# One PSUM bank for the modulation fold, others for gathers and a norm sum, and a reordered router stage, in a two-block transformer kernel on one core

## The chip, the core and the metric

The kernel runs as one program on one core of a Trainium2 chip. The metric is the device time of one execution in microseconds (us); lower is better. TensorE multiplies into eight PSUM banks of 128 partitions by 512 float32 values, VectorE, ScalarE and GpSimd work beside it, and weights are brought from HBM by DMA transfers, nearly all of them issued in order from one queue (SyncE's, "SPq" in the profile). In the profile PE is TensorE's matmul, PEld its weight load, DVE is VectorE, ACT is ScalarE, POOL is GpSimd.

## The reference

Two transformer blocks on 256 tokens of width 1024, then a norm. The change lies wholly in the first block, in two places of it: the attention and the router.

```python
mod = jax.nn.silu(c) @ w_ada[l] + b_ada[l]
shift1, scale1, gate1, shift2, scale2, gate2 = jnp.split(mod[:, None, :], 6, axis=-1)
...
y_na = neighbourhood_attention(qa, ka, va, na_rpb[l])
...
y_mla = blocked_full_attention(qm, km, vm)
...
x = x + gate1 * (merged @ w_out[l])
h2 = rms_norm(x, g_norm2[l]) * (1.0 + scale2) + shift2
# moe_ffn: 64 experts, 8 chosen for each token
scores = jax.nn.sigmoid((t @ w_router).astype(jnp.float32))
...
routed = lax.map(expert_chunk, (tc, gc)).reshape(T, D)
shared = (jax.nn.silu(t @ w_sg) * (t @ w_su)) @ w_sd
```

The modulation `mod` is a product of one vector with a 1024 x 6144 matrix; the experts' weights are 64 times three 1 MB matrices.

## The kernel before

Each engine's program is written out by hand, one function for each engine, and each engine runs its own program strictly in order. Nothing is scheduled by a planner: the order in the code is the order on the engine. What ties the engines together are semaphores.

**Banks.** `open_group(name, b)` on TensorE waits until the bank `b` has been emptied by whoever reads its last group, and takes it. `close_group` marks the group full, `full(engine, name)` makes an engine wait for that, and `emptied(instruction, name)` gives the bank back. So a bank number is a wait: a group opened in a bank whose last reader is late stops TensorE, and all that is queued behind it. `done(engine, name)` waits for the same release.

**Weights.** A ring of 11 slots of 1 MB holds weight slabs. `take_slab` waits for the next one; `ends(n, group)` says with which group's end a slot is free, and SyncE's queue then issues the next load into it. The loads are in one fixed order. The slabs of the experts that are sorted by load come after a wait for `ordered`, which VectorE sets once it has copied out the sorted list of experts (L2331). The first two expert units and the slabs before them don't need it.

**Attention** (`early_attention`, L637 to L671). `scores(0)`, `ada_fold(1)`, `scores(1)`, four slabs of modulation product (L493, 16 instructions each), and then eight times: scores two pairs ahead (L610), two transposes `turn` of the probabilities (L626), two more slabs of modulation product, and the values product of the pair before (L640). Each pair is two heads. `ada_fold` (L520 to L526) turns a quarter-summed row of the modulation into columns with four short matmuls. The scores of pair 0 go to banks 0 and 1, those of pair 1 to banks 5 and 7, those of pair 2 to 0 and 1 again. VectorE takes for every head the row maximum of the scores (`na_scores`, L2167 and L2172), and later scales the exponentials by their sum (L2097, L2100). Its own order is: maxima of pair 0, `ada(1)` (L1983, which reads the fold and frees its bank), maxima of pair 1, scaling of pair 0, maxima of pair 2, scaling of pair 1, and so on. GpSimd makes the bias of each head ahead of its maximum (L1545): that of head h starts when the scores of head h - 2 have been read.

**Router** (L926 to L1034 on TensorE, L2237 to L2375 on VectorE). The router's logits are summed in `rtT`, copied out transposed (`rtS`, L2240) and turned back (`rt`, bank 7, L949 and L951). `row_sums` gives each token's norm, `two_sums` (L543, L545) gives the same sums broadcast over partitions (`sum2`). `turn_rows` (`tk`, four groups in banks 1 to 4) turns the activations for the gathers; VectorE empties them in `rest_of` (L2252, 0.7 us each). From the sigmoid scores VectorE works out the mask of the chosen experts (L2256 to L2285), the counts, the sorting matrix `perm`, the list of experts, and each token's place. `shared("shg", ...)` is the gate product of the shared expert, 16 steps in two groups: banks 0 and 7. It depends on none of the sorting and stands between the sorting's short matmuls. `gather(0, 0)` to `gather(0, 3)` (L1021) fetch the tokens of the first two expert units, and ScalarE evicts them (L1792). `unit(0)` starts the experts; its first group `gu` opens bank 5 (L1189).

## Time and profile before

| | us |
|---|---|
| three timed runs | 1097.80, 1099.66, 1099.83 |
| their median | 1099.66 |
| the profiled execution's own time | 1099.61 |
| its span in the profile | 1097.8 |
| mean granted TensorE clock | 0.991 of full |

The span is 1.8 us shorter than the time of the same execution; that rest lies around the span and is taken as fixed. The page of the profile shows PE busy for 1055.3 us of the span, DVE 394.4, ACT 286.6, POOL 54.0, and DMA at 421 GB/s in most slices between 329 and 823 us. In a timeline row the columns are start, length, engine, line, operation, output and inputs, shape, count, and in brackets the idle time before it and what released it. Float32 matmuls show twice in such a row: a product of two float32 tiles counts two.

### The profile page before, as it was taken

The page shows a single profiled execution, that of the slowest core. Times are in us where ns is not written, and L with a number is a line of the kernel's source. Part 1 is how long each engine was busy: PE and PEld are TensorE (multiplying, and loading weights), DVE is VectorE, ACT ScalarE, POOL GpSimd, SP SyncE. Part 2 cuts the span into 40 slices and gives each one's busy share as a digit, 9 for nine tenths or more (in the row PEclk, how much of TensorE's full clock was granted, in tenths as well). Part 3 has the DMA queues.
Part 4 walks back from the last instruction along what each step waited for, and adds up shares of the span by engine and source line. Part 5 has one row for each costly group of instructions (what it writes and reads, how often), then busy time and mean ns, then how long its engine had stood idle before and what let it go on. Part 6 is the DMA issues. An engine that isn't in the chain of part 4 may idle for free.

```text
span 1097.8 us, 15950 instructions
## 1 busy us (share of the span) xinstructions
PE 1055.3 (96%) x6296; PEld 726.0 (66%) x6296; DVE 394.4 (36%) x1034; ACT 286.6 (26%) x658; POOL 54.0 (5%) x87
## 2 busy tenths in 40 slices
PE   6999999999999998999899999999889999999998
PEld 4786775688755654665356655655458888887567
DVE  1298976523532232112112122122333021523841
ACT  3124145511431121122111121113222111213951
POOL 0000202013100000000000000001000001100001
PEclk9999999999999999999989999999999999999999
DMA  9999387965599999999999999999997334310000
GB/s 384 338 420 421 148 349 283 421 261 194 213 350 423 421 420 420 420 421 420 421 420 421 407 421 421 420 421 421 418 417 282 125 116 154 115 39 1 1 2 38
DMA packets 49611, 335.12 MB, mean 305 GB/s; under 512 B 5472, under 2 KB 7872, under 8 KB 9984
## 3 DMA queue, kind: packets, MB, share of 16 engines
q1 hardware_dynamic: 46976, 329.01, 73.7%
q10 hardware_dynamic: 2176, 3.37, 1.0%
q0 software_dynamic: 384, 1.70, 0.4%
q8 instruction: 51, 0.84, 0.3%
q14 instruction: 24, 0.20, 0.0%
HBM read 333.02 MB, written 1.05 MB: 304 GB/s over the span
## 4 chain that ended last, share of the span: by engine, by line
PE 90%; DMA 4%; DVE 4%; ACT 1%; issue 1%; SPq 0%; DVEq 0%; ACTq 0%
PE bank L1189 14%; PE bank L574 10%; PE bank L1232 7%; PE bank L1144 5%; PE bank L1331 5%; PE bank L1021 4%; DMA ring<-experts 4%; PE bank L1043 3%; PE bank L493 3%; PE bank L1081 3%; PE bank L1419 3%; PE bank L901 3%; PE bank L1374 3%; PE bank L917 3%; PE bank L704 2%; PE bank L640 2%
## 5 line engine op out<-in xcount | busy, mean ns | idle before, releaser
L1189 PE MATMUL bank<-ring,arena 128*32 128x512 f32 (+1 forms) x1112 | 176.9, 605 | 11.3 <-DMA ring<-experts 10.7
L1189 PEld LDWEIGHTS bank<-ring,arena 128*32 128x32 f32 (+1 forms) x1112 | 52.3, 121 | 115.4 <-issue 115.3
L574 PE MATMUL bank<-hT,ring 128*128 128x256 f32 x512 | 113.0, 381 | 0.7 <-ACT hT L1622 0.7
L574 PEld LDWEIGHTS bank<-hT,ring 128*128 128x128 f32 x512 | 96.5, 190 | 18.1 <-issue 5.4
L1232 PE MATMUL bank<-ring,conds 128*32 128x512 f32 (+1 forms) x560 | 89.1, 608 | 5.1 <-DMA ring<-experts 3.4
L2475 DVE TENSOR_TENSOR yhalf<-bank,yhalf 128x512 fp32r<-128x512 f32 x48 | 33.2, 691 | 80.7 <-ACT yhalf L1831 80.7
L1792 ACT ACTIVATE arena<-bank,mod 128x256 f32<-128x256 f32 x96 | 40.3, 471 | 81.3 <-PE bank L1021 81.2
L1232 PEld LDWEIGHTS bank<-ring,conds 128*32 128x32 f32 (+1 forms) x560 | 27.4, 121 | 49.1 <-issue 44.3
L1556 POOL TENSOR_TENSOR hT<-hT 128x256 f32<-128x256 f32 x30 | 21.7, 724 | 744.1 <-ACT hT L1616 742.6
L2460 DVE SCALAR_TENSOR_TENSOR conds<-bank,gcol,conds 128x256 f32<-128x256 f32 x24 | 11.6, 484 | 129.4 <-ACT conds L1823 118.7
L1021 PE MATMUL bank<-picked,halves 128*128 128x256 f32 x384 | 57.5, 292 | 0.4 <-ACT arena L1792 0.4
L1331 PE MATMUL bank<-hT,ring 128*128 128x256 f32 x256 | 57.0, 379 | 0.0
L1021 PEld LDWEIGHTS bank<-picked,halves 128*128 128x128 f32 x384 | 48.6, 188 | 10.3 <-issue 9.1
L2225 DVE SCALAR_TENSOR_TENSOR resid<-bank,mod,resid 128x256 f32<-128x256 f32 (+1 forms) x48 | 19.7, 437 | 93.8 <-PE bank L1419 25.8
L1331 PEld LDWEIGHTS bank<-hT,ring 128*128 128x128 f32 x256 | 48.3, 190 | 6.6 <-issue 0.2
L1823 ACT ACTIVATE conds<-bank 128x256 f32<-128x256 f32 x24 | 9.2, 383 | 155.1 <-PE bank L1189 155.1
L1043 PE MATMUL bank<-yhalf,selT 128*128 128x512 f32 x192 | 48.5, 394 | 0.0
L1831 ACT CAST yhalf<-bank 128x512 fp32r<-128x512 f32 x48 | 28.1, 585 | 61.4 <-PE bank L1232 61.4
L1144 PE MATMUL bank<-hT,ring 128*128 128x256 f32 x192 | 43.2, 382 | 0.0
L2051 DVE SCALAR_TENSOR_TENSOR arena<-ring,conds,arena 128x256 f32<-128x256 f32 x84 | 40.7, 485 | 3.0
L1616 ACT ACTIVATE hT<-resid 128x256 f32<-128x256 f32 x48 | 17.9, 413 | 89.6 <-DVE resid L2225 89.6
L1144 PEld LDWEIGHTS bank<-hT,ring 128*128 128x128 f32 x192 | 36.0, 190 | 7.2 <-issue 2.5
(423 smaller groups left out, 1506.9 us busy)
## 6 DMA issues: line engine op xcount, KB each, us to landing
ring<-experts SPq DMA_DIRECT2D x187, 1024.0 KB, 13.8
ring<-stream SPq DMA_DIRECT2D x118, 1024.0 KB, 11.8
ring<-experts SPq DMA_DIRECT2D x8, 512.0 KB, 11.3
resid<-x SPq DMA_DIRECT2D x1, 1024.0 KB, 5.2
resid<-ctx ACTq DMA_DIRECT2D x1, 1024.0 KB, 10.0
keys_room<-experts SPq DMA_DIRECT2D x1, 1024.0 KB, 7.0
arena<-stream SPq DMA_DIRECT2D x1, 1024.0 KB, 7.9
hT<-stream SPq DMA_DIRECT2D x1, 1024.0 KB, 8.0
```

The lines of the kernel that those rows point to most:

```text
L493: mm = mmul(o[32 * g:32 * g + 32, 0:256], (silc if which == "ada1" else silc2)[:, 4 * kk + g, at:at + 32], w[:, 4 * kk + g, :], start=firs ...
L574: mm = mmul(o[:, 0:n_tok], w[:, k, t * P:(t + 1) * P], hT[:, k, 0:n_tok], start=(k == 0), stop=(k == KT - 1))
L901: mm = mmul(o[:, 0:256], w[:, 512 * k + P * t:512 * k + P * t + P], yT[:, y0 + k, :], start=(k == 0), stop=(k == 3))
L1021: mm = mmul(o[:, 256 * (d % 2):256 * (d % 2) + n], halves[:, q, t, P * d:P * d + P], picked[:, t, 0:n], start=(t == 0 and q == 0), stop=(t ...
L1043: mm = mmul(bank[b][:, :], selT[:, b // 2, :], yhalf[:, q, 512 * (b % 2):512 * (b % 2) + 512], start=m == 0 and q == 0, stop=last and q == 1)
L1144: mm = mmul(o[:, 0:T], w[:, k, P * (i % 2):P * (i % 2) + P], hT[:, k, T:2 * T], start=(k == 0), stop=(k == KT - 1))
L1189: mm = mmul(o[at:at + n_slots, :], xg_of(m, kk)[:, at:at + n_slots], w[g][:, k, :], start=(kk == 0), stop=(kk == KT - 1))
L1232: mm = mmul(o[at:at + n_slots, :], aT[:, f, at:at + n_slots], w[g][:, 2 * c + f, :], start=(f == 0), stop=(f == 1))
L1331: mm = mmul(o[:, 0:T], eight(n)[:, k, (i % 2) * P:(i % 2 + 1) * P], hT[:, k, 0:T], start=(k == 0), stop=(k == KT - 1))
L1792: last = a.activation(to[:, i, 0:n], bk(("xg", j, c))[:, 256 * i:256 * i + n], ACT.Identity, bias=mod1[:, 24 + 2 * c + i:25 + 2 * c + i])
L2051: last = v.scalar_tensor_tensor(out=at, in0=w[:, k, :], scalar=silc[:, k, 15:16], in1=at, op0=ALU.mult, op1=ALU.add)
L2475: last = v.tensor_tensor(yhalf[:, 1, 512 * c:512 * c + 512], bk(("y", m, c))[:, :], yhalf[:, 0, 512 * c:512 * c + 512].bitcast(F32), ALU.s ...
```

## The change

Six edits, in the first block only. No instruction is added or removed.

- `ada_fold(1)` opens bank 3 in place of bank 7.
- On VectorE the copy of the router's logits (`rtS`) stands ahead of the reciprocal of the row norms, not behind it.
- `sum2` opens bank 7 in place of bank 0, behind `rt`, which is in bank 7 too; its eviction `mean("n2", ...)` moves from ahead of the mask's work to behind it.
- The shared gate products no longer stand ahead of the counts; they are cut 3, 2, 3 in place of 4, 2, 2, and the second group stands between the second and third gather in place of ahead of the first.
- The four first gathers open banks 1, 3, 4, 2 in place of 4, 5, 4, 5; the turn of the gates stands behind the third gather, their sorting behind the fourth.
- On VectorE `rest_of(0)` moves behind the counts, and the work on the shared product (`by_row`, `by_token`) behind that on the sorted gates.

```diff
-            def ada_fold(batch):
+            def ada_fold(batch, b=7):
...
-                o = open_group((batch, "columns"), 7)
+                o = open_group((batch, "columns"), b)
...
-                ada_fold(1)
+                ada_fold(1, 3)
...
-            two_sums("sq2", "sum2", 0)
+            two_sums("sq2", "sum2", 7)
...
-            shared("shg", 0, 0, range(0, 4))
             pe.wait_ge(S("mask"), 1)
...
-            shared("shg", 0, 0, range(4, 6))
+            shared("shg", 0, 0, range(0, 3))
...
-            shared("shg", 0, 0, range(6, KT))
+            shared("shg", 0, 0, range(3, 5))
             sort_by_rank("slots_by_rank", "slots_by_expert", 0, 5)
-            shared("shg", 1, 7, range(0, KT))
-            ends(ng, ("shg", 1))
-            pe.wait_ge(S("gates_made"), 1)
-            turn_by_expert("gates_by_expert", gates)
+            shared("shg", 0, 0, range(5, KT))
...
-                o = open_group(name, 5 if j == 0 and c % 2 else 4)
+                o = open_group(name, (1, 3, 4, 2)[c] if j == 0 else 4)
...
             gather(0, 0)
             gather(0, 1)
+            shared("shg", 1, 7, range(KT))
+            ends(ng, ("shg", 1))
             gather(0, 2)
+            pe.wait_ge(S("gates_made"), 1)
+            turn_by_expert("gates_by_expert", gates)
+            gather(0, 3)
             sort_by_rank("gates_by_rank", "gates_by_expert", 1, 6)
-            gather(0, 3)
...
+            full(dve, "rtT")
+            emptied(v.tensor_copy(rtS, bk("rtT")[:, 0:T + 1]), "rtT")
             done(dve, "row_sums")
             link(v.reciprocal(row_rms[:, :], row_rms[:, :]))
-            full(dve, "rtT")
-            emptied(v.tensor_copy(rtS, bk("rtT")[:, 0:T + 1]), "rtT")
...
-            mean("n2", "sum2", at=1)
...
-            rest_of(0)
+            mean("n2", "sum2", at=1)
```

On TensorE, at the start of the attention, this is the place of `ada_fold(1)` (L525) between the scores of pair 0 and pair 1 (L610), with the bank releases that each waits for:

```order
 L610 MATMUL bank<-arena 128x256 [waits psum_done1]
 L610 MATMUL bank<-arena 128x256 x2
-L525 MATMUL bank<-cs,quarters 128x32 [waits psum_done7,psum_done6]
+L525 MATMUL bank<-cs,quarters 128x32 [waits psum_done3,psum_done6]
 L525 MATMUL bank<-cs,quarters 128x32
 L610 MATMUL bank<-arena 128x256 [waits psum_done5]
```

Only the bank of the fold differs; the scores of pair 1 still open banks 5 and 7 behind it.

On TensorE, behind the logits' turn `rt` (L951), this is the broadcast norm sum `sum2` (L543, L545):

```order
 L949 MATMUL bank<-cs,pr 128x64
 L951 MATMUL bank<-cs,pr 128x64
-L543 MATMUL bank<-hT,ones 128x256 [waits sq2_part,psum_done0]
+L543 MATMUL bank<-hT,ones 128x256 [waits sq2_part,psum_done7]
 L545 MATMUL bank<-hT,ones 128x256 [waits sq2]
 L942 MATMUL bank<-cs,arena 128x128 [waits psum_done3]
```

It now waits for the release of bank 7, which `rt` has just filled.

On TensorE, from the counts (which end just ahead of the first row) to the first expert unit, before: L966 is the shared gate product, L998 and L999 the order, L986 a turn by expert, L993 a sorting product, L1021 a gather (8 rows each).

```order
L966 MATMUL bank<-arena,ring 128x257 x2
L998 MATMUL bank<-pr,cs 1x64
L999 MATMUL bank<-pr 1x64
L986 MATMUL bank<-cs,pT 64x128 x2
L966 MATMUL bank<-arena,ring 128x257 x2
L993 MATMUL bank<-pr,arena 128x64 x2
L966 MATMUL bank<-arena,ring 128x257 x8
L986 MATMUL bank<-cs,pr 64x128 x2
L1021 MATMUL bank<-picked,halves 128x256 x24
L993 MATMUL bank<-pr,arena 128x64 x2
L1021 MATMUL bank<-picked,halves 128x256 x8
```

The same place in the changed kernel, whose line numbers are lower by one to four:

```order
L966 MATMUL bank<-arena,ring 128x257 x3
L997 MATMUL bank<-pr,cs 1x64
L998 MATMUL bank<-pr 1x64
L985 MATMUL bank<-cs,pT 64x128 x2
L966 MATMUL bank<-arena,ring 128x257 x2
L992 MATMUL bank<-pr,arena 128x64 x2
L966 MATMUL bank<-arena,ring 128x257 x3
L1017 MATMUL bank<-picked,halves 128x256 x16
L966 MATMUL bank<-arena,ring 128x257 x8
L1017 MATMUL bank<-picked,halves 128x256 x8
L985 MATMUL bank<-cs,pr 64x128 x2
L1017 MATMUL bank<-picked,halves 128x256 x8
```

The eight steps of the second shared group moved behind two gathers, and the gates' turn behind the third.

## Rows read from the trace of the kernel before

**Rows 1.** The page: the chain that ended last, shares by engine.

```profile
PE 90%; DMA 4%; DVE 4%; ACT 1%; issue 1%; SPq 0%; DVEq 0%; ACTq 0%
```

**Rows 2.** The page: GB/s moved in 40 slices of 27.4 us each.

```profile
GB/s 384 338 420 421 148 349 283 421 261 194 213 350 423 421 420 420 420 421 420 421 420 421 407 421 421 420 421 421 418 417 282 125 116 154 115 39 1 1 2 38
```

**Rows 3.** Timeline of PE at the start of the attention.

```profile
173.40 0.70 PE L610 MATMUL bank<-arena 64*128 64x256 f32 x2
175.38 1.47 PE L610 MATMUL bank<-arena 64*128 64x256 f32 x6 [1.28 <-DVE mod L1983]
176.78 4.95 PE L493 MATMUL bank<-ring,conds 128*32 128x256 f32 x64
181.66 1.14 PE L610 MATMUL bank<-arena 64*128 64x256 f32 x8
182.72 1.10 PE L626 MATMUL bank<-cs,pr 128*128 128x128 f32 x8
183.75 1.93 PE L493 MATMUL bank<-ring,conds 128*32 128x256 f32 x32
...
187.13 1.38 PE L626 MATMUL bank<-cs,pr 128*128 128x128 f32 x8 [0.39 <-DVE pr L2100]
```

**Rows 4.** Timeline of DVE in the same stretch.

```profile
178.43 1.37 DVE L2100 TENSOR_SCALAR pr<-pr,att 128x256 f32<-128x256 f32 x2
...
179.91 0.62 DVE L2100 TENSOR_SCALAR pr<-pr,att 128x256 f32<-128x256 f32 x2
183.42 0.42 DVE L2167 CUSTOM_DVE_ANT_0 pr<-bank,bias_room 128x256 f32<-128x256 f32 x1 [2.89 <-PE bank L626]
```

**Rows 5.** Timeline of POOL in the same stretch.

```profile
173.89 2.59 POOL L1545 TENSOR_TENSOR bias_room<-bias_room,cs 128x256 f32<-128x256 f32 x4 [46.19 <-DVE att L2167]
176.98 2.67 POOL L1545 TENSOR_TENSOR bias_room<-bias_room,cs 128x256 f32<-128x256 f32 x4 [0.51 <-DVE att L2167]
```

**Rows 6.** Stretches: busy us of PE, PEld, DVE, ACT, POOL, granted clock, DMA share, GB/s.

```profile
176.00:178.00 2.00, 2.00 (x16) 0.73 (x17) 1.80 (x10) 1.22 (x5) 1.50 (x3) 0.51 0.73 307
181.00:223.00 42.00, 41.02 (x446) 25.76 (x440) 23.81 (x85) 25.10 (x74) 4.83 (x7) 1.00 1.01 417
286.00:288.00 2.00, 2.00 (x10) 1.80 (x9) 1.35 (x12) 1.31 (x3) 0.00 (x0) 0.50 1.00 414
323.00:324.00 1.00, 1.00 (x12) 0.26 (x9) 0.42 (x1) 0.55 (x1) 0.00 (x0) 1.00 0.07 16
```

**Rows 7.** Timeline of PE from the logits' turn to the first expert unit.

```profile
284.17 0.66 PE L949 MATMUL bank<-cs,pr 128*128 128x64 f32 x4 [0.52 <-DVE pr L2240]
...
284.89 0.80 PE L543 MATMUL bank<-hT,ones 128*128 128x256 f32 x2
...
292.48 2.01 PE L966 MATMUL bank<-arena,ring 128*128 128x257 f32 x8
294.32 0.33 PE L973 MATMUL bank<-pT,ones 128*128 128x64 f32 x2
...
296.86 0.27 PE L998 MATMUL bank<-pr,cs 64*1 64x64 f32 x2
...
298.97 3.75 PE L966 MATMUL bank<-arena,ring 128*128 128x257 f32 x16
...
308.88 0.64 PE L1189 MATMUL bank<-keys_room,arena 128*64 128x512 f32 x1 [0.93 <-ACT arena L1792]
```

**Rows 8.** Timeline of DVE in the router.

```profile
283.69 0.43 DVE L2240 COPY pr<-bank 128x257 f32<-128x257 f32 x1
...
285.35 0.48 DVE L2244 SCALAR_TENSOR_TENSOR pT<-bank,row_rms,pT 128x64 f32<-128x64 f32 x2
...
292.54 0.29 DVE L2285 TENSOR_TENSOR pT<-pT 128x128 f32<-128x128 f32 x1
...
299.40 0.76 DVE L2314 TENSOR_TENSOR picked<-cs,pr 128x256 fp32r<-128x256 f32 x2
```

**Rows 9.** Timeline of SyncE's DMA queue, the first loads behind `ordered`.

```profile
298.49 51.51 SPq L1477 DMA_DIRECT2D ring<-experts  x25
```

15 lines of the change are left out of this document (8 added, 7 removed).

## The prediction

> **What bounds the kernel now.** I read the page first: the chain that ended last is 90% PE and 4% DMA [rows 1], so a microsecond is won only where PE waits or where the stream of expert slabs is let go earlier; that stream runs at 420 GB/s from the 13th slice to the 30th [rows 2], 329 to 823 us. PE itself stands still at the two places that the change touches, so I read those stretches as timelines, engine by engine. In the attention PE issues two instructions of the scores of pair 1 and then stands until 175.38 for VectorE's read of the fold, L1983 [rows 3]: the fold and the scores of head 3 share bank 7. Right behind it the granted clock is 0.51 of full between 176 and 178 [rows 6], the 1.2 GHz level, and the 64 instructions of modulation product take 4.88 us (176.78 to 181.66), where 32 at full clock have a length of 1.93 [rows 3]. From 181 to 223 PE is busy 41.0 of 42 us at full clock [rows 6]: once this start is over, PE bounds the attention. In the router PE stands 0.52 us for the copy of the logits, and 0.93 us for the last eviction of a gather ahead of the first expert unit [rows 7].
>
> **The fold in bank 3.** The bank was last used by an early sum, long read. Eight L610 in a row take 1.06 us start to start (181.66 to 182.72), so the 64 of L493 start at 173.40 + 1.07 = 174.47 in place of 176.78: 2.31 us earlier. If the half-clock stretch goes with the idle time that stood ahead of it, they take 2 x 1.93 less the overlap, 3.72 in place of 4.88: 1.16 us more. PE is at the next scores at 178.19 and at the first turn (L626) at 179.25, against 182.72 [rows 3]. Now VectorE must be looked at, which had slack of 2.89 us there [rows 4]. The turn needs the scaled probabilities of head 0, L2100, which ended at 178.43 + 1.37 = 179.80. VectorE gets pair 1's scores at once, but GpSimd's bias of head 3 is ready only at 173.89 + 2.59 = 176.48 [rows 5]. Before, VectorE began head 3 right behind its release of head 2, at which GpSimd's next bias started, 176.98 [rows 5]; so it gains 0.5 to 0.6 us, no more. The scaling of head 0 is then over at about 179.25, that of head 1 at 180.53 - 0.6 = 179.95 [rows 4]. VectorE goes on with pair 2's maxima at 179.95, which started at 183.42: 3.47 us earlier. From there its work is the same row after row, and at 187.13 PE was waiting for exactly this chain [rows 3]; so PE comes out 3.47 us ahead at most, and on its own path (second turn at 180.05, over at 180.6, L493 at 180.6 against 183.75) 3.15 us. If VectorE gained nothing on heads 0 and 1, pair 2 would start at 180.55: 2.87. **Term 1: 3.4 us, from 2.9 to 3.5.**
>
> GpSimd matters for this: the first pair of L2100 took 1.37 us and the second 0.62 [rows 4], and the first ended 0.15 us after GpSimd's last bias (176.98 + 2.67 = 179.65) [rows 5]. The Trainium skill, page "SBUF — State Buffer", section "Who interferes with whom", has a rule for it: a VectorE scalar operation in its two-port mode and a GpSimd instruction exclude each other. The trace agrees with it here. By that rule the scaling of head 0 cannot end before GpSimd's does, which moves ahead by only 0.5 us (176.98 to 176.48); without it head 0 would be scaled at 178.5 and term 1 would be at its upper end, 3.5.
>
> The slabs bear it: each load is issued when PE frees the slot 11 slabs earlier, so the issues move with PE, and PE met no missing slab in this stretch while the DMA ran at 417 GB/s [rows 6].
>
> **The logits' copy and bank 7.** The logits are full before PE turns to the norms; the copy L2240 stood behind a reciprocal that waits for ScalarE, and started at 283.69 [rows 8]. Ahead of it, it needs nothing but the logits, so PE's pause of 0.52 ahead of `rt` goes, with the restart behind it 0.6 us. `rt` starts at 283.55, and VectorE's L2244, which ended at 285.35 + 0.48 = 285.83, ends at about 285.2 [rows 7, 8]. PE loses this again at once: `sum2` shares bank 7 with `rt` and waits for L2244. It starts at 285.25, where it started at 284.89 [rows 7]. PE's idle time here grows from 0.52 to about 0.85, and PE is 0.36 us **behind**. Queued behind that wait are the other turns and four modulation slabs; ScalarE's first parts, which hang on them, have slack. **Term 2: 0.36 us lost, from 0.1 to 0.6.**
>
> **The mask.** The scores reach VectorE 0.6 us earlier, and the mean (0.6 us with its signal; it used to wait for `sum2` as well) no longer stands ahead of them. The mask, ready at 292.54 + 0.29 = 292.83 [rows 8], is ready at about 291.4. PE comes out of the modulation slabs at 292.48 + 0.36 = 292.84 and starts the counts there, 1.48 us earlier than at 294.32 [rows 7], without waiting for the mask. The mean and `rest_of(0)` fit in VectorE's waits for the counts and for the order; uncovered they would cost 0.6 and 0.7 us.
>
> **The order.** From the counts to the order 2.54 us passed (294.32 to 296.86) with two shared steps between; now there are three, at 1.84 / 4 = 0.46 us each (292.48 to 294.32 holds four) [rows 7]. Less a pause of 0.1 the order is at 292.84 + 2.54 + 0.46 - 0.1 = 295.74. So the expert loads start not at 298.49 [rows 9] but at 297.4: 1.1 us earlier, on top of term 1.
>
> **The gathers.** Counts, order, the first eight shared steps and the first sorting took 292.48 to 298.97, 6.49 us [rows 7]. It is the same work in another order, less some 0.2 of pauses for VectorE: PE is ready to gather at 299.1. `picked` ended at 299.40 + 0.76 = 300.16 [rows 8] and hangs on the sorting, which is 1.1 us earlier: 299.05, just in time. From there on every bank is free: 1, 3, 4 and 2 are those of the turned activations, which `rest_of` has emptied by 300.4, and bank 5 of the first expert group was read long before, so the 0.93 us ahead of L1189 are gone. The whole stretch from 292.48 to 308.88 was 16.40 us [rows 7]; less 0.93 and 0.3 of pauses it is 15.17, and L1189 starts at 308.0. **Terms 2 to here together: 0.9 us won, from 0.5 to 1.1.** Two things run later than before and are costed at nothing. The work on the shared product ends on VectorE at about 312; the hidden values of unit 0, the next thing that waits for VectorE or ScalarE, come after 315, and beyond these 3 us each one costs one. The last shared step, and with it the slot of its slab, is over at about 305.0 in place of 302.7 (298.97 + 3.75) [rows 7]; the five expert loads issued before it, 5 MB at 420 GB/s, keep the DMA busy until 310.
>
> **Does it reach the end?** The last gap of the expert stream is at 323 to 324, with 16 GB/s [rows 6], and it ends with a slot that PE frees in unit 0. From there the stream runs full up to 823 [rows 2], and the 4% of DMA in the chain [rows 1] are PE's waits for it. Its start moves with PE, so all behind moves by the whole sum: 3.4 + 0.9 = 4.3 us. From the profiled execution's own time: 1099.61 - 4.3 = **1095.3**; the median of the runs (1099.66) is the same within 0.05.
>
> **Rivals.**
> *Half clock stays.* The clock may fall in the attention though the wait is gone, or a wait of 0.5 us for VectorE at the first turns brings it back. For it: the clock is low again at 286 to 288 [rows 6], where PE was busy but with short work behind 0.52 us of idle time. Against it: 42 us of the same mix at full clock [rows 6]. Then PE is at the first turn at 180.4 and term 1 is about 1.3 to 2.3; with 0.9: 1099.61 - 2.2 to 3.2, say 1096.9. A rule of the Trainium skill stands beside it (page "TensorE: Matmul & The Clock Gate", section "What's actually happening"): the half rate is the default and activity lifts it. No run here shows yet how much activity the start of the attention has without the wait.
> *Absorbed.* Term 1 is eaten between 224 and 282 or by slabs that land late. Against it: PE is busy 41.0 of 42 us up to 223, and loads are let go by PE itself, so they move with it [rows 6]. Then only 0.9 is left: 1098.7.
> *Slower.* The clock is the mechanism, its places the early turns that now wait for VectorE and the router stage, where the new wait for bank 7 stands in a stretch already at 0.50 [rows 6]. Each further half-speed stretch costs 1.16 us, as above; the fourth eats the gain, and six give 1099.61 - 4.3 + 7.0 = 1102.3.
> *More.* The half-clock stretch at 286 falls elsewhere: 1.2 us better, 1094.1.
>
> **How the numbers follow.** Forecast as worked out 0.70 (its own range 1094.3 to 1096.4), half clock stays 0.14, absorbed 0.07, slower 0.04, more 0.05. About 0.2%, 2.2 us, is what a measurement of this kernel can tell from no change, so faster means below 1097.4: 0.70 + 0.05 + half of the 0.14, 0.82. Same: 0.14. Slower: 0.04. The range takes in the ends of the terms, the half-clock case and the better case, 1093.9 to 1097.8.
>
> **What would show it.** PE's L610 at 173.40 as one row of eight with no bracket; clock 1.00 in 176 to 178; pair 2's maxima near 180; each row from 183.75 on 3.4 us earlier, up to the router; there a wait of 0.8 ahead of L543 for VectorE's L2244, no wait ahead of L1189, the expert loads 4.5 us earlier than at 298.49. It is wrong if the clock falls in the attention, if the turns wait for VectorE at every pair, or if PE's waits for slabs grow by what was won.

## The result, and the profile after

| | before | after |
|---|---|---|
| median of the compared runs | 1099.09 | 1093.48 |
| lowest and highest of them | 1097.80 to 1099.83 (5) | 1090.61 to 1095.00 (5) |
| ratio, 95% interval | | 0.9948, 0.9934 to 0.9962 |
| the profiled execution's own time | 1099.61 | 1090.61 |
| its span | 1097.8 | 1088.8 |

The kernel after is 5.6 us faster by the medians. Predicted were 1095.3 us with a range from 1093.9 to 1097.8: the side was right, and the time came out 0.4 us below the range. The profiled execution of after is the fastest of its five, so it shows a span that is 9.0 us shorter; what of these 9.0 us belongs to the change has to be sorted out first.

The page of after, where the chain that ended last stood in [rows 1]:

```profile
PE 88%; DMA 6%; DVE 4%; issue 1%; ACT 1%; SPq 0%; DVEq 0%; ACTq 0%
```

PE still makes most of the chain, and the stream of expert slabs is as full as before: the page of after has 405 to 422 GB/s in the slices that had 407 to 423 in [rows 2]. The attention, in the timeline of PE of after (start, length, engine, line, shape, count, and in brackets the idle time ahead):

```profile
171.72 0.63 PE L525 MATMUL bank<-cs,quarters 128*128 128x32 f32 x4
172.28 1.13 PE L610 MATMUL bank<-arena 64*128 64x256 f32 x8
173.34 3.66 PE L493 MATMUL bank<-ring,conds 128*32 128x256 f32 x64
176.94 1.13 PE L610 MATMUL bank<-arena 64*128 64x256 f32 x8
178.23 1.38 PE L626 MATMUL bank<-cs,pr 128*128 128x128 f32 x8 [0.16 <-DVE pr L2100]
179.54 1.93 PE L493 MATMUL bank<-ring,conds 128*32 128x256 f32 x32
...
183.95 1.29 PE L493 MATMUL bank<-ring,conds 128*32 128x256 f32 x20
```

The eight L610 are one row without a bracket, where [rows 3] had two rows with 1.28 us of idle time between; the 64 products of L493 take 3.60 us to the next row (173.34 to 176.94) in place of 4.88. The fold L525 started at 172.84 in the trace of before and at 171.72 here. Those 1.12 us lie ahead of everything that the change touches: they belong to the execution, not to the change (over the fourteen traces of all kernels the fold starts between 171.40 and 173.07). Measured from the fold on, PE is 3.09 us ahead at the first L493 behind the turns (183.75 to 179.54) and 3.37 us ahead from the second on, at 183.95. In the trace of before that one is

```profile
188.44 1.93 PE L493 MATMUL bank<-ring,conds 128*32 128x256 f32 x32
```

In the timelines of VectorE and GpSimd of after, what answers to [rows 4] and [rows 5]:

```profile
176.81 1.35 DVE L2100 TENSOR_SCALAR pr<-pr,att 128x256 f32<-128x256 f32 x2
...
178.92 0.42 DVE L2167 CUSTOM_DVE_ANT_0 pr<-bank,bias_room 128x256 f32<-128x256 f32 x1
...
172.78 5.24 POOL L1545 TENSOR_TENSOR bias_room<-bias_room,cs 128x256 f32<-128x256 f32 x8 [46.18 <-DVE att L2167]
```

GpSimd's two biases are now one unbroken row that ends at 178.02, and the first scaling ends at 178.16, 0.14 us behind it, as it did before (0.15). It is long again (1.35 us, the next one 0.62). What the Trainium skill says on the page "SBUF — State Buffer", section "Who interferes with whom", fits this trace as it fitted the one before.

The stretches of after that answer to [rows 6] (busy us of PE, PEld, DVE, ACT, POOL, granted clock, DMA share, GB/s):

```profile
176.00:178.00 2.00, 2.00 (x28) 1.04 (x20) 1.93 (x6) 1.65 (x7) 2.00 (x4) 1.00 1.00 393
...
282.00:284.00 2.00, 2.00 (x31) 1.49 (x32) 1.86 (x16) 1.73 (x3) 0.00 (x0) 1.00 1.00 411
286.00:288.00 2.00, 1.86 (x27) 1.24 (x16) 1.70 (x12) 1.23 (x3) 0.00 (x0) 1.00 0.84 290
```

The stretch at half clock in the attention is gone, and the one in the router (0.50 in 286 to 288 before) is gone too, which the forecast had not counted. The router, in the timeline of PE of after, to be held against [rows 7]:

```profile
278.52 0.64 PE L942 MATMUL bank<-cs,arena 128*128 128x128 f32 x4
278.99 0.56 PE L949 MATMUL bank<-cs,pr 128*128 128x64 f32 x4
...
280.67 0.70 PE L543 MATMUL bank<-hT,ones 128*128 128x256 f32 x2 [0.90 <-DVE pT L2244]
...
283.04 3.66 PE L493 MATMUL bank<-ring,conds 128*32 128x256 f32 x64
286.84 0.41 PE L972 MATMUL bank<-pT,ones 128*128 128x64 f32 x2
...
301.52 0.64 PE L1189 MATMUL bank<-keys_room,arena 128*64 128x512 f32 x1
```

The pause of 0.52 ahead of L949 is gone, the new wait ahead of L543 is there (0.90; 0.85 was expected), and L1189 starts without one. From the first turn L942 to L1189 it is 23.00 us; before, the turn started at 283.02 and L1189 at 308.88 [rows 7], 25.86. On VectorE the mask's last instruction is

```profile
286.44 0.29 DVE L2284 TENSOR_TENSOR pT<-pT 128x128 f32<-128x128 f32 x1
```

and ends at 286.73, 0.11 us ahead of the counts L972: PE has just come out of the slabs and takes the mask as it comes. The first load behind `ordered`, on SyncE's queue, stood at 298.49 in [rows 9]. Now it is at

```profile
291.52 1.48 SPq L1477 DMA_DIRECT2D ring<-experts  x2
```

Behind the router the traces of before and after take the same time for 500 us (308.88 to 804.26, and 301.52 to 796.86: 495.38 and 495.34 us), though not step by step. 33 us behind L1189 PE waits for a slab in after, and doesn't at the same step in before. First before, then after:

```profile
341.57 3.65 PE L1189 MATMUL bank<-ring,arena 128*64 128x512 f32 x16
```

```profile
334.80 3.65 PE L1189 MATMUL bank<-ring,arena 128*64 128x512 f32 x16 [0.53 <-DMA ring<-experts]
```

And before has half clock from 549 to 555 (granted 0.51), after only from 542 to 546 (0.57), about 1.7 us more of lost clock that the time doesn't show: PE waits for slabs in this part anyway, 5.25 and 5.23 us at the start of these stretches. At the end of the 500 us PE waits for the last late slab, 3.43 us in both. First before, then after:

```profile
804.26 5.22 PE L1232 MATMUL bank<-ring,conds 128*32 128x512 f32 x32 [3.43 <-DMA ring<-experts]
```

```profile
796.86 3.64 PE L1232 MATMUL bank<-ring,conds 128*32 128x512 f32 x32 [3.43 <-DMA ring<-experts]
```

In the stretch from 804 to 808 of before the granted clock is 0.57, in that from 796 to 800 of after 1.00; this gives another 1.58 us. So the 9.0 us between the two traces are 1.1 of an earlier start, 3.4 in the attention, 2.9 in the router and 1.6 behind the last late slab. The experiments were made to tell which of these the change brings in every execution.

### The profile page after: what moved, and what is told of

It reads as the page before. It is cut to its first block, busy times and chain, and to the rows that moved or that the text cites. A ratio compares the mean times of both kernels' runs of the same rounds, so it can differ in the third digit from the quotient of the medians.

```text
span 1088.8 us, 15949 instructions
## 1 busy us (share of the span) xinstructions
PE 1047.4 (96%) x6296; PEld 723.9 (66%) x6296; DVE 394.9 (36%) x1034; ACT 286.4 (26%) x658; POOL 53.5 (5%) x87
## 3 DMA queue, kind: packets, MB, share of 16 engines
q10 hardware_dynamic: 2176, 3.37, 1.1%
## 4 chain that ended last, share of the span: by engine, by line
PE 88%; DMA 6%; DVE 4%; issue 1%; ACT 1%; SPq 0%; DVEq 0%; ACTq 0%
PE bank L1189 14%; PE bank L574 10%; PE bank L1232 7%; PE bank L1144 5%; PE bank L1331 5%; DMA ring<-experts 5%; PE bank L1017 4%; PE bank L1043 3%; PE bank L1081 3%; PE bank L1419 3%; PE bank L901 3%; PE bank L917 3%; PE bank L1374 3%; PE bank L493 3%; PE bank L704 2%; PE bank L640 2%
## 5 line engine op out<-in xcount | busy, mean ns | idle before, releaser
L1189 PE MATMUL bank<-ring,arena 128*32 128x512 f32 (+1 forms) x1112 | 176.0, 602 | 11.6 <-DMA ring<-experts 10.4
L1189 PEld LDWEIGHTS bank<-ring,arena 128*32 128x32 f32 (+1 forms) x1112 | 52.5, 120 | 114.8 <-issue 114.7
L1232 PE MATMUL bank<-ring,conds 128*32 128x512 f32 (+1 forms) x560 | 87.5, 595 | 5.6 <-DMA ring<-experts 3.9
L1232 PEld LDWEIGHTS bank<-ring,conds 128*32 128x32 f32 (+1 forms) x560 | 27.5, 119 | 47.9 <-issue 42.7
```

The lines of the kernel that those rows point to most:

```text
L1189: mm = mmul(o[at:at + n_slots, :], xg_of(m, kk)[:, at:at + n_slots], w[g][:, k, :], start=(kk == 0), stop=(kk == KT - 1))
L1232: mm = mmul(o[at:at + n_slots, :], aT[:, f, at:at + n_slots], w[g][:, 2 * c + f, :], start=(f == 0), stop=(f == 1))
```

## Experiments

Every kernel was run beside runs of the kernel before on the same chip. In the table, "attention" is the time from the fold (L525) to the L493 behind the second turns, 172.84 to 188.44 before; "router" is the time from the first L942 to the first L1189; "to the last slab" is the time from that same first L942 to the L1232 that waits for the last late slab. "Half" says that a stretch at half clock lay in the part. Each of these three is from one traced execution.

| kernel | mean, us (runs) | ratio to before, 95% | attention, us | router, us | to the last slab, us |
|---|---|---|---|---|---|
| before | 1098.52 (77) | | 15.60, half | 25.86, half | 521.24 |
| after | 1093.36 (5) | 0.9948, 0.9934 to 0.9962 | 12.23 | 23.00 | 518.34 |
| after, again | 1092.83 (6) | 0.9952, 0.9935 to 0.9969 | 12.24 | 23.01 | 518.36 |
| fold only | 1094.51 (7) | 0.9968, 0.9952 to 0.9984 | 12.22 | 24.20 | 519.20 |
| all but the fold | 1097.75 (12) | 0.9995, 0.9986 to 1.0005 | 15.60, half | 24.52, half | 519.99 |
| wait filled | 1096.16 (12) | 0.9978, 0.9967 to 0.9989 | 13.99 | 24.21 | 520.69 |
| gathers' banks only | 1098.19 (12) | 0.9995, 0.9981 to 1.0009 | 13.98 | 24.61, half | 521.63 |
| sum2 in bank 0 | 1094.02 (9) | 0.9961, 0.9945 to 0.9978 | 12.21 | 23.01 | 518.53 |
| router wait filled | 1093.99 (6) | 0.9957, 0.9941 to 0.9972 | 12.22 | 23.00 | 520.09 |
| order held back | 1093.82 (6) | 0.9953, 0.9936 to 0.9969 | 12.21 | 22.99 | 520.88 |
| gathers' banks undone | 1096.53 (10) | 0.9988, 0.9971 to 1.0005 | 12.24 | 24.69 | 519.93 |
| copy behind again | 1093.58 (9) | 0.9957, 0.9943 to 0.9970 | 12.23 | 25.00, half | 522.32 |
| sum2 behind the turns | 1092.79 (7) | 0.9956, 0.9939 to 0.9974 | 12.22 | 22.12 | 518.38 |
| fold and gathers' banks | 1094.63 (6) | 0.9952, 0.9935 to 0.9970 | 12.22 | 22.92 | 520.56 |

Executions of one and the same kernel lie 2 to 8 us apart. Over the 77 of before, time and mean granted clock go together: those with a clock of 0.988 took 1099.8 to 1102.2 us, those with 0.995 to 0.997 took 1093.8 to 1096.6, and a straight line through all of them has 0.8 us for each 0.001. So a mean of six or so is good to about 0.7 us, and the parts of the attention and the router are read from the traces. There they repeat to 0.03 us where the code and the clock are the same. The last column doesn't: after and the kernel with the router's wait filled agree in the router to 0.01 and differ by 1.75 us at the last slab.

### The kernel after once more

The changed kernel itself, run again.

> The changed kernel once more, for a second trace and a tighter time. Theory A: 5 to 6 us faster than before; the trace shows full clock from the logits' turn to the counts again. Rival C (the clock there falls by chance in either kernel, and the first trace was a lucky one): 4.3 us, ratio 0.9961, and a half-speed stretch somewhere between the norms and the counts.

Its mean is 1092.83, and with the first five runs 1093.07 over eleven, 5.4 us below the 1098.52 of before. In its trace the router takes 23.01 us, again without half clock: theory A held. The fastest two of the eleven (1090.61 and 1090.64) explain nothing about the change; the trace of after happens to be of the first of them.

### The fold alone

```diff
-            def ada_fold(batch):
+            def ada_fold(batch, b=7):
...
-                o = open_group((batch, "columns"), 7)
+                o = open_group((batch, "columns"), b)
...
-                ada_fold(1)
+                ada_fold(1, 3)
```

> The kernel before with the fold in bank 3 alone. Theory A (the two parts add up, the attention as predicted, the router more than predicted because its half-speed stretch goes as well): 3.4 us faster than before, ratio 0.9969, and the half-speed stretch near 286 us of before is still there, moved with the work. Rival B (the attention was under-sized and gives the rest of the 5.6 us): 4.5 us or more, ratio 0.9959 or less. In the trace both expect eight L610 in one row and full clock in the 64 L493 behind them; the first L626 within 0.3 us of VectorE's L2100.

The timeline of PE of this kernel, in the attention and in the router:

```profile
172.43 0.63 PE L525 MATMUL bank<-cs,quarters 128*128 128x32 f32 x4
...
174.05 3.66 PE L493 MATMUL bank<-ring,conds 128*32 128x256 f32 x64
...
279.21 0.64 PE L942 MATMUL bank<-cs,arena 128*128 128x128 f32 x4
280.37 0.66 PE L949 MATMUL bank<-cs,pr 128*128 128x64 f32 x4 [0.52 <-DVE pr L2240]
...
287.00 2.01 PE L966 MATMUL bank<-arena,ring 128*128 128x257 f32 x8
...
303.41 0.64 PE L1189 MATMUL bank<-keys_room,arena 128*64 128x512 f32 x1 [0.93 <-ACT arena L1792]
...
336.10 3.65 PE L1189 MATMUL bank<-ring,arena 128*64 128x512 f32 x16
```

The attention is as in the kernel after: from the fold on, PE is 3.38 us ahead of before at the L493 behind the second turns (188.44 to 184.65). And the router, whose code is that of before, with the same 0.52 and 0.93 us of idle time, ran at full clock: 24.20 us in place of 25.86. The stretch at half clock costs 1.66 us when it falls there, and the router's waits alone don't bring it. Theory A had the attention right and the router's clock wrong. The times by themselves don't decide: the interval, 0.9952 to 0.9984, holds the 0.9969 of A and the 0.9959 of B.

### All but the fold

The kernel after with the fold back in bank 7:

```diff
-                ada_fold(1, 3)
+                ada_fold(1)
```

> The changed kernel with the fold back in bank 7, so the router's edits alone. Theory A: 0.9 us by the terms and up to 1.6 us more where the half-speed stretch in the router is gone: 0.9 to 2.5 us faster, ratio 0.9992 to 0.9977. Rival B: 0.9 us, ratio 0.9992, with the half-speed stretch as before.

The mean is 0.77 us below that of before, and the interval of the ratio takes in 1. In the trace the router takes 24.52 us with a stretch at half clock in it (L543 takes 1.17 us for two instructions, L942 2.30 for twelve, where after has 0.70 and 1.47), against 25.86 of before with one: 1.34 us at half clock. At full clock it is 24.20 less 23.00, 1.20. The prediction had 0.9 for this. By time and clock this is rival B: the stretch stayed.

### The attention's wait filled

The kernel before, with four idle products into bank 3, which nobody reads, between the fold and the scores of pair 1, so that PE works while it used to stand:

```diff
                 scores(0)
                 ada_fold(1)
+                done(pe, "mq_sums")
+                for _ in range(4):
+                    mmul(bank[3][:, 0:256], ones[:], hT[:, 0, 0:256], start=True, stop=True)
                 scores(1)
```

> The kernel before with four idle products of 128 x 256 (into bank 3, read by nobody) between the fold and the scores of pair 1, so that TensorE still may not go on before VectorE has read the fold, but works through most of that wait. If the idle time is what brings the half-speed stretch, the 64 L493 behind it take 3.7 us in place of 4.9 and the kernel is about 1.2 us faster than before (ratio 0.9989). If the clock falls there for another reason (short products of 32 and 64 columns), they still take 4.9 us and the time is that of before.

The timeline of PE of this kernel:

```profile
172.89 0.63 PE L525 MATMUL bank<-cs,quarters 128*128 128x32 f32 x4
173.36 1.97 PE L662 MATMUL bank<-hT,ones 128*128 128x256 f32 x8
175.26 1.30 PE L610 MATMUL bank<-arena 64*128 64x256 f32 x8
176.50 3.66 PE L493 MATMUL bank<-ring,conds 128*32 128x256 f32 x64
180.09 1.14 PE L610 MATMUL bank<-arena 64*128 64x256 f32 x8
```

The scores of pair 1 come hardly earlier than before (2.37 us behind the fold, before 2.54), and yet the 64 products take 3.59 us, not 4.88: here the clock stayed up. From the fold to the next scores it is 7.20 us in place of 8.82. So of the 3.4 us of the attention 1.6 are the clock, and the rest is the wait itself. The router, with its code unchanged, took 24.21 us at full clock, as in the kernel with the fold alone.

This one trace does not show that the idle time was what brought the clock down, since the clock also stayed up once with the wait unfilled (the next kernel, 13.98 us in the attention against 13.99 here). The times show it: by its own 24 runs of before, this kernel is 2.3 us faster (1.2 to 3.6 by the interval), though it does no work earlier than the unfilled wait at full clock does. Filling the wait raises the clock on average; what it saves in a single execution differs.

### The banks of the gathers alone

```diff
-                o = open_group(name, 5 if j == 0 and c % 2 else 4)
+                o = open_group(name, (1, 3, 4, 2)[c] if j == 0 else 4)
```

> The kernel before with the four first gathers in banks 1, 3, 4, 2 and nothing else. The wait of 0.93 us ahead of the first L1189 goes, and the 0.2 us ahead of the third gather: from the first turn to L1189 24.2 us at full clock become 23.1 to 23.3. The kernel is 0.9 to 1.1 us faster than before, ratio 0.9991. If this is all that the router's edits bring at full clock (1.2 us), the early counts and the early order bring next to nothing; if L1189 starts 0.9 us earlier but the time doesn't move, the stream of expert loads is what holds the end.

By its times it can't be told from before (0.9995). The trace tells more. Its attention first, whose code is that of before:

```profile
171.41 0.63 PE L525 MATMUL bank<-cs,quarters 128*128 128x32 f32 x4
...
173.96 1.13 PE L610 MATMUL bank<-arena 64*128 64x256 f32 x6 [1.29 <-DVE mod L1983]
175.01 3.66 PE L493 MATMUL bank<-ring,conds 128*32 128x256 f32 x64
178.60 1.14 PE L610 MATMUL bank<-arena 64*128 64x256 f32 x8
...
185.39 1.93 PE L493 MATMUL bank<-ring,conds 128*32 128x256 f32 x32
```

The wait is there as in before, 1.29 us, and the 64 products behind it run at full clock, in 3.59 us. So this stretch at half clock isn't a fixed part of the kernel before either. It costs 15.60 - 13.98 = 1.62 us when it falls there, and the fold's edit is worth 13.98 - 12.22 = 1.76 us when it doesn't.

In the router there is a stretch at half clock, so only the part behind it is taken, from the shared steps L966 to L1189:

```profile
289.39 2.01 PE L966 MATMUL bank<-arena,ring 128*128 128x257 f32 x8
...
304.57 0.64 PE L1189 MATMUL bank<-keys_room,arena 128*64 128x512 f32 x1
...
338.46 3.65 PE L1189 MATMUL bank<-ring,arena 128*64 128x512 f32 x16 [1.14 <-DMA ring<-experts]
```

That is 15.18 us; the kernel with the fold alone, also at full clock, has 287.00 to 303.41, 16.41. The banks bring 1.23 us: 0.99 from the last gather to L1189 (1.14 in place of 2.13), and 0.24 in the gathers ahead of it (3.00 us to the next row in place of 3.24). But 34 us further on PE waits 1.14 us for a slab, where before and the kernel with the fold alone don't wait. From the first turn to this step it is 58.50 us here and 58.55 in before (283.02 to 341.57), both with one stretch at half clock in the router: nearly all that the banks won is gone again.

### The norm sum in bank 0

The kernel after with `sum2` back in bank 0, free of the wait for VectorE's L2244:

```diff
-            two_sums("sq2", "sum2", 7)
+            two_sums("sq2", "sum2", 0)
```

> The changed kernel with sum2 back in bank 0, so that TensorE doesn't stand 0.90 us for VectorE ahead of it. Theory A (at full clock the mask, not TensorE, is the last to be ready for the counts): L543 starts about 0.9 us earlier, but the counts start with the mask as before, and L1189 is at most 0.2 us earlier counted from the first turn; the time is that of the changed kernel within 0.4 us. Rival (the wait for bank 7 is a loss on the path, 0.36 us by the prediction, and brings the half-speed stretch): 0.4 to 2 us faster than the changed kernel.

The timeline of PE of this kernel:

```profile
279.27 0.65 PE L543 MATMUL bank<-hT,ones 128*128 128x256 f32 x2
...
286.50 0.41 PE L972 MATMUL bank<-pT,ones 128*128 128x64 f32 x2 [1.25 <-issue]
```

L543 starts without a wait, PE is through with the slabs 1.1 us earlier, and then it stands 1.25 us ahead of the counts for the mask. The router takes 23.01 us, as in after. At full clock the wait for bank 7 costs nothing in this order, since the mask ends last. Theory A held in the trace; the mean is 0.95 us above after's, inside the scatter.

### The router's wait filled

The kernel after with two idle products into bank 0 ahead of `sum2`; nobody reads them:

```diff
+            done(pe, ("pn", 6))
+            for _ in range(2):
+                mmul(bank[0][:, 0:256], ones[:], hT[:, KT - 1, 0:256], start=True, stop=True)
             two_sums("sq2", "sum2", 7)
```

> The changed kernel with two idle products of 128 x 256 (into bank 0, read by nobody) in the wait ahead of sum2. They fit into that wait and move nothing. If idle time in the router is what brings the half-speed stretch in some executions, the granted clock averaged over the runs is higher than the changed kernel's 0.9934 (up to 0.995) and the time 0.5 to 1.5 us lower. If not, clock and time are those of the changed kernel.

The router takes 23.00 us and the mean is 1093.99, within the scatter of after's 1093.07. The wait of 0.90 us is filled and no gain follows. Behind this wait the clock stayed full in four traces without the filler (after, after again, order held back, gathers' banks undone) and fell in two (all but the fold, copy behind again), so that this one trace at full clock doesn't tell whether filling it keeps the clock up. The mean granted clock over the six runs is 0.9937, after's over eleven 0.9934; the times say that it is worth less than their scatter.

### The order held back

The kernel after with VectorE's signal `ordered` given some 4 us later:

```diff
-            v.tensor_copy(order[0:1, 0:E], bk("order")[0:1, 0:64]).then_inc(S("ordered"), 1)
+            link(v.tensor_copy(order[0:1, 0:E], bk("order")[0:1, 0:64]))
...
             choose(0)
+            v.memset(order[0:1, E:E + 1], 0).then_inc(S("ordered"), 1)
```

> The changed kernel with the signal that lets the sorted expert loads go held back on VectorE by about 4 us, behind the last split of the turned activations; nothing else waits for it. Theory A (the stream's start doesn't count, since the loads soon stand still for ring slots and the last gap ends with a slot that TensorE frees in unit 0): the first loads start 4 us later, the gap near 306 to 316 us shrinks, and the time is that of the changed kernel within 0.5 us. Rival (the early order is part of the gain): up to 4 us slower than the changed kernel.

The first load behind it, on SyncE's queue, is at

```profile
295.96 1.49 SPq L1477 DMA_DIRECT2D ring<-experts  x2
```

in a trace in which the router starts 0.44 us later than in after, so it is held by 4.0 us. The mean is 1093.82, 0.75 above after's and inside the scatter; the 4 us that the rival allowed are out, and nothing that can be measured hangs on the earlier expert loads. In its one trace PE waits 0.84 us at the slab where after waited 0.53 and after again 0.33, which is too little to tell from the scatter there.

### The banks of the gathers undone

```diff
-                o = open_group(name, (1, 3, 4, 2)[c] if j == 0 else 4)
+                o = open_group(name, 5 if j == 0 and c % 2 else 4)
```

> The kernel after with one edit undone: the four first gathers open banks 4, 5, 4, 5 again. Measured between the first turn (L942) and the first product of the expert units (L1189), which took 23.00 us in the kernel after at full clock and 24.20 in the kernel before with only the fold moved, also at full clock. Theory A (the banks are the largest part of the 1.2 us: the last gather and L1189 share bank 5, and L1189 waits for ScalarE's eviction): L1189 waits 0.8 to 1.0 us again, the stretch is 23.8 to 24.0 us, the other router edits are worth 0.2 to 0.4. Theory B (the new order of the gathers hides the eviction by itself, since the sorting of the gates stands between): the stretch is below 23.4 us. Both: time between the kernel before and the kernel after, ratio 0.995 to 0.998.

The timeline of PE of this kernel, the kernel after with the old banks:

```profile
295.13 2.14 PE L1017 MATMUL bank<-picked,halves 128*128 128x256 f32 x16 [1.00 <-DVE halves L2251]
...
303.77 0.64 PE L1189 MATMUL bank<-keys_room,arena 128*64 128x512 f32 x1 [0.34 <-ACT arena L1792]
```

Both expectations missed the place. L1189 waits only 0.34 us (theory B had that right), but a wait of 1.00 us stands ahead of the first gather: bank 4 holds the turned activations that VectorE empties last, in `rest_of(3)`, behind the picked slots. In the order of after the shared steps no longer cover that. The router takes 24.69 us, 1.69 more than in after: with the new order the banks are worth more than with the old one (1.23), because bank 1 is the first to be emptied and the first to be opened. The mean of the times is 3.5 us above after's, more than the 1.69; its mean clock was lower too (0.992 against 0.993), and the rest is not explained.

### The copy behind the reciprocal again

```diff
-            full(dve, "rtT")
-            emptied(v.tensor_copy(rtS, bk("rtT")[:, 0:T + 1]), "rtT")
             done(dve, "row_sums")
             link(v.reciprocal(row_rms[:, :], row_rms[:, :]))
+            full(dve, "rtT")
+            emptied(v.tensor_copy(rtS, bk("rtT")[:, 0:T + 1]), "rtT")
```

> The kernel after with one edit undone: on VectorE the logits' copy stands behind the reciprocal of the row norms again. Theory A (the mask's chain is what PE waits for at the counts, and it starts with this copy): copy at the reciprocal's end, 0.6 to 0.7 us later; the turn rt, the mask and the counts are later by as much, and the stretch from the first turn to L1189 is 23.6 to 23.7 us in place of 23.00. Theory B (the copy is paid back by PE's wait for bank 7, as the prediction's sum had it: PE comes to the counts on its own path): the counts are not later by more than 0.3 us, 23.0 to 23.3.

The wait of 0.52 us ahead of L949 is back, as in [rows 7]. The trace is no clean answer: it has a stretch at half clock in the router, which takes 25.00 us, where the two others at half clock that have the copy early or the gathers' banks have 24.52 and 24.61. This execution took 1098.8 us at a clock of 0.990. The other eight took 1091.4 to 1093.4 at 0.993 to 0.995, and the median is 1093.12. Ahead of the stretch L543 starts 2.86 us behind the first turn, in after 2.15, so that on PE's own path the copy is not paid back there, against theory B. What is left of these 0.71 us at L1189 at full clock isn't measured; the times, with a mean 0.5 us above after's, leave no room for more than about 1 us. The other eight, some 5 us faster than the one in the trace, were not traced; that the time between lies in such stretches is read from their mean clock alone.

### The fold and the gathers' banks

The kernel before with these two edits and nothing else; its diff is that of the fold alone and that of the gathers' banks alone.

> The kernel before with two of the six edits: the fold in bank 3, and the four first gathers in banks 1, 3, 4, 2. The router's code, the norm sum's bank, the place of the logits' copy and of the shared steps are those of before. Theory A (the banks of the fold and of the gathers carry the whole gain): at full clock the stretch from the first turn to the first product of the expert units is 24.20 - 1.23 = 22.97 us (24.20 with the fold alone; 1.23 is what the gathers' banks took off from the shared steps on, 15.18 against 16.41), the same as the kernel after's 23.00, and the time is the kernel after's, some 1093.1. Theory B (the copy and the reordered shared steps carry a part of their own): the stretch is above 23.3 us. If the stretch at half clock falls in the router, both are 1.5 us more there.

The timeline of PE of this kernel:

```profile
279.27 0.63 PE L942 MATMUL bank<-cs,arena 128*128 128x128 f32 x4
...
302.19 0.64 PE L1189 MATMUL bank<-keys_room,arena 128*64 128x512 f32 x1
...
336.61 3.65 PE L1189 MATMUL bank<-ring,arena 128*64 128x512 f32 x16 [1.30 <-DMA ring<-experts]
```

Theory A held: 22.92 us (22.97 was expected) against 23.00 of after. Up to L1189 the two edits that change a bank number do all that the six do; the early copy, the wait for bank 7 and the moved shared steps cancel out. Behind it they don't: PE waits 1.30 us for a slab here, and 0.32 one step earlier, where after waits 0.53. From the first turn to this step it is 57.34 us, against 56.28 in after and 56.89 with the fold alone (279.21 to 336.10). In this trace, as in that of the gathers' banks alone, the slabs take back what the banks won. That the other edits, the moved shared steps for one, are what spares after most of this wait would fit, but no experiment separates them. By its own runs of before (mean 1099.29) the kernel is 4.7 us faster, which six runs don't tell from after's 5.4.

### The norm sum behind the turns

A version meant to beat both: the kernel after with `sum2` behind the three other turns, when VectorE has long emptied bank 7, and the time so won filled with shared steps:

```diff
-            two_sums("sq2", "sum2", 7)
             turn_rows(2, 3)
             turn_rows(1, 2)
             turn_rows(3, 4)
+            two_sums("sq2", "sum2", 7)
...
+            shared("shg", 0, 0, range(0, 2))
             pe.wait_ge(S("mask"), 1)
...
-            shared("shg", 0, 0, range(0, 3))
+            shared("shg", 0, 0, range(2, 5))
...
-            shared("shg", 0, 0, range(3, 5))
+            shared("shg", 0, 0, range(5, 7))
...
-            shared("shg", 0, 0, range(5, KT))
+            shared("shg", 0, 0, range(7, KT))
+            shared("shg", 1, 7, range(0, 2))
...
-            shared("shg", 1, 7, range(KT))
+            shared("shg", 1, 7, range(2, KT))
```

> The kernel after with the norm sum sum2 behind the three turns that stood behind it (bank 7 still), so that VectorE has emptied bank 7 when PE comes to it, and with the time that this frees filled: two steps of the shared gate product ahead of the wait for the mask, and the first two steps of the second group ahead of the first gather. Nothing is added or left out. Theory A (PE's 0.90 us of idle time at sum2 is lost time that only looks free because the mask is waited for next): PE stands nowhere between the first turn and the counts, and the stretch from the first turn to L1189 is 22.0 to 22.3 us in place of 23.00, 0.7 to 1.0 us won on the kernel after; ratio to before about 0.994. Theory B (VectorE's chain from the mask over the counts and the order to the picked slots sets the gathers, and the shared steps moved ahead only make room for waits behind): 22.8 to 23.1 us.

The timeline of PE of this kernel:

```profile
287.05 0.43 PE L973 MATMUL bank<-pT,ones 128*128 128x64 f32 x2 [0.18 <-DVE pT L2286]
...
300.90 0.64 PE L1191 MATMUL bank<-keys_room,arena 128*64 128x512 f32 x1
...
334.66 3.65 PE L1191 MATMUL bank<-ring,arena 128*64 128x512 f32 x16 [1.01 <-DMA ring<-experts]
```

PE now stands 0.18 us from the first turn (278.78) to the counts, and the router takes 22.12 us, 0.88 less than in after: theory A held in the router. But the wait for the slab is 1.01 us here, 0.53 in after, and at the last late slab nothing is left: 518.38 us from the first turn, 518.34 in after. The mean of the times is 1092.79, 0.3 us below after's. That is the lowest mean of all, but it is not shown that this kernel is faster than after.

## Why the prediction was right and wrong

**The fold: right against the trace of before.** Predicted 3.4 us (2.9 to 3.5), measured 3.37 in after and 3.38 with the fold alone. Each step is there: 3.60 us for the 64 products (3.72), VectorE's gain on the first two heads and its tie to GpSimd, pair 2's maxima 3.4 us earlier once the start is taken off (183.42 - 1.12 - 178.92 = 3.38), the slabs on time. But 1.6 us of it are the stretch at half clock, which the sum took as a fixed part of before. It isn't: with the wait in place the clock fell in two traces (before, all but the fold) and not in the third (gathers' banks alone), where the fold's edit would bring 1.76. That idle time and clock are tied was argued; the filled wait shows it by its mean, 2.3 us.

**Bank 7: size right, its meaning not.** Predicted 0.36 us lost. From the first turn to the end of the slabs the fold-only kernel took 7.79 us at full clock (279.21 to 287.00), and after needs 8.11 (278.52 to 286.63, the start of its 64 products plus the 3.59 us that they take in both): 0.32 lost. But the sum took the mask to be ready 1.4 us before PE. That came from PE's arrival in the trace of before, with 1.66 us of half clock in it. The mask itself came as forecast: 1.6 us earlier, counted from the first turn (9.81 to 8.21), where 1.4 was said. At full clock PE arrives when the mask does (286.63 and 286.73), and without the wait for bank 7 it stands 1.25 us for the mask instead.

**The step that failed, in the terms: what the gathers and the pauses bring.** From the end of the slabs to L1189 the sum took off 0.93 for the last eviction and 0.3 for pauses, 1.23. Measured at full clock: 16.41 with the fold alone, 14.89 in after (286.63 to 301.52), so 1.52. The 0.93 were right, the pauses were 0.59. The new banks alone bring 1.23, 0.24 of it ahead of the last gather, and 0.29 come with the new order of the shared steps. With the loss of 0.32 this gives 1.20 for the router, where 0.9 was said, with 1.1 as its upper end.

**The step that failed, in the chances: the half clock in the router.** It was read from one trace, taken as a fixed part of the router, and that it could fall elsewhere got 5 in 100, as the rival "more". In the fourteen traces it is there in before, in the gathers' banks alone, in all but the fold and in the copy behind again; it is not there in the other ten, of after twice. It doesn't look like chance alone: all three traces with the idle wait in the attention have it, and of the eleven without that idle time ten have full clock in the router, those with its code unchanged too. Why a wait in the attention should matter 110 us later is open. So the likeliest case was the better one, worth up to 1.66 us, and together with the pauses and the base it puts the result below the range.

**What adds up.** The wait itself is worth 1.76 us in the attention, and the edits in the router 1.20 up to L1189, both at full clock. For the clock the filled wait gives a price: its attention and router take the time of the unfilled ones at full clock (13.99 and 13.98; 24.21 and 24.20), and its mean is 2.3 us lower. That makes 5.3 us, and the means show 5.4 (1098.52 to 1093.07). The sum fits, but it is argued: the 2.3 are known to between 1.2 and 3.6, and which stretches they lie in was seen in one execution only. Nor do all stretches cost time: the second one of before at 549 to 555 us doesn't, as shown above.

**The way to the end.** The prediction had all behind the router move by the whole sum, and called it wrong if PE's waits for slabs grew by what was won. In part they did. Against the fold alone, after is 1.20 us ahead at L1189 and 0.61 us 33 us later (56.89 to 56.28), with 0.53 of wait between. At the last late slab it is 0.86 (519.20 to 518.34) and in after again 0.84, but single traces of nearly one kernel differ by 1.75 us there. With the gathers' banks over the router of before, alone and with the fold, the waits were 1.14 and 1.30 us and took back what the banks had won. So a gain in the router is no forecast of the time, and its 1.20 us are an upper end.

**The base.** The sum was made from a profiled execution of 1099.61 us. Over 77 runs the mean of before is 1098.52, so that execution was 1.1 us slow itself. Had the forecast stood on that mean, it would have been 1094.2. Its two errors, 1.1 us too high a base and 1.1 us too small a gain, add up, and are what is between 1095.3 and 1093.1. The 1.8 us between span and time, taken as fixed, are 1.8 in four of the five runs of after and 2.7 in one.

**The range** reached down to a case with everything going well, 1093.9, with nothing for the scatter of executions, which is 4.4 us from the lowest to the highest of the five of after.

**The order** was predicted 4.5 us earlier and came 7.0 earlier, 5.8 without the earlier start, of which 1.7 are the half clock of the router in before; holding it back by 4.0 changed nothing that could be measured. That the gain would come through PE, as the sum had it, was right.

## What to carry to other kernels

Where banks are handed on by hand, list for each bank when its last reader ends, and open first the one that is emptied first: here the fold's bank alone brings 3.9 of the 5.4 us by the means, and two bank numbers did up to the end of the router what six edits did. Then follow the gain past the place where it was made: a step won ahead of a stream of weights can be lost again in the next wait for a slab. When PE's arrival at a wait is read from a trace, look at the granted clock ahead of it: a stretch at half clock makes the engine look late, and hides that it will wait once the clock is up. And look at the unchanged parts of every trace that was taken for something else: that the wait in the attention doesn't always cost the clock shows only in the trace of the gathers' banks. Before forecasting a few us, get more than three runs of the kernel before, and place the profiled execution among them.

## What the runs showed of the hardware

Stretches at half clock come and go between executions, even of one program. In the first trace of after PE ran at full clock from 427 to 430 us, in the second at half:

```profile
427.00:430.00 3.00, 3.00 (x32) 0.94 (x24) 0.00 (x0) 0.00 (x0) 0.00 (x0) 1.00 1.00 415
```

```profile
427.00:430.00 3.00, 3.00 (x16) 0.83 (x20) 0.00 (x0) 0.00 (x0) 0.00 (x0) 0.50 1.02 423
```

Idle time makes them likelier, as the 2.3 us of the filled wait show, but does not decide. Behind the 1.28 us of idle time in the attention the clock fell in two traces of three, and in none of the eleven with the time filled or the wait removed. Behind the last late slab, where the code is the same in all kernels and PE had waited 2.9 to 3.6 us, it fell in nine of fourteen: 5.22 us for 32 products in before, 3.64 in after, behind the same wait of 3.43 us.

A stretch costs 1.6 to 1.7 us where PE is the bound (15.60 for 13.98 in the attention, 25.86 for 24.20 in the router, 5.22 for 3.64 behind the last late slab) and nothing that shows where PE waits for slabs anyway (495.38 and 495.34 us from L1189 to the last late slab, with two and one such stretches at 542 to 555).

The start of a program differs between executions too: the fold, with nothing changed ahead of it, began between 171.40 and 173.07 us in the fourteen traces.
